# Three output projections from high and low parts, modulation chunks in value jobs, a bias pair ahead, the last expert reordered

## What is computed

```python
for i in range(DEPTH):                      # first block: 32 experts, top 2, FF 256
    h = rms_norm(x, norm1_g[i])             # i=0 gated MLP mixer, i=1 latent attention
    ...
    x = x + jnp.concatenate([mix, mem_out], axis=-1) @ w_out      # 1536 x 1024
    x = x + hierarchical_moe(rms_norm(x, norm2_g[i]), ...)
for i in range(DEPTH):                      # second block: 16 experts, FF 256
    mod = (silu(c) @ w_ada[i] + b_ada[i]).reshape(b, 6, d)
    sh_m, sc_m, g_m = mod[:, 0, None, :], mod[:, 1, None, :], mod[:, 2, None, :]
    sh_f, sc_f, g_f = mod[:, 3, None, :], mod[:, 4, None, :], mod[:, 5, None, :]
    hm = rmsnorm(x, norm_mix[i]) * (1 + sc_m) + sh_m
    # i=0 dilated mixer (w_in 1024 x 9216), i=1 forgetting mixer (w_in 1024 x 3088)
    x = x + g_m * (attention_output @ w_out)                      # 1024 x 1024
    hf = rmsnorm(x, norm_ffn[i]) * (1 + sc_f) + sh_f
    x = x + g_f * hierarchical_moe_2(hf, ...)
```

## Time and profile before

| | us |
|---|---|
| median of 3 runs | 1722.71 |
| lowest, highest | 1720.19, 1725.01 |
| the profiled execution | 1724.17 |
| its span | 1722.4 |
| PE busy in it | 1565.0 (91%) |
| DVE busy | 812.5 (47%) |
| ACT busy | 506.7 (29%) |
| POOL busy | 135.8 (8%) |

### The profile page before, as it was taken

The page is one execution under the profiler, slowest core; times in us unless marked ns, Lnnn a source line. Parts: engine busy times, 40 slices in busy tenths (PEclk is TensorE's granted clock), DMA queues, the critical chain, the costliest instruction groups (busy, mean ns, idle before and its releaser), DMA issues. The chain is left out here.

```text
span 1722.4 us, 23229 instructions
## 1 busy us (share of the span) xinstructions
PE 1565.0 (91%) x8906; PEld 986.1 (57%) x8906; DVE 812.5 (47%) x1862; ACT 506.7 (29%) x1016; POOL 135.8 (8%) x158
## 2 busy tenths in 40 slices
PE   6899899999699798999979988997899979889997
PEld 3487455554375555555437766776565537646553
DVE  0647343333433636333236745664663336576433
ACT  1222121111215412111116555654222125641211
POOL 0000201010000002010001001000021001002110
PEclk9899999999899999999999989998989989998999
DMA  9785559999872083999996350335357993616794
GB/s 358 259 340 217 199 237 420 421 421 421 359 285 106 4 366 132 421 420 421 420 425 252 147 202 24 142 121 222 123 222 314 421 390 122 244 73 273 286 420 199
DMA packets 62107, 467.23 MB, mean 271 GB/s; under 512 B 7664, under 2 KB 15776, under 8 KB 17184
## 3 DMA queue, kind: packets, MB, share of 16 engines
q1 hardware_dynamic: 61984, 465.59, 66.9%
HBM read 462.81 MB, written 2.76 MB: 270 GB/s over the span
## 5 line engine op out<-in xcount | busy, mean ns | idle before, releaser
L1528 PE MATMUL PS<-ring,catT 128*64 128x256 f32 x3072 | 368.5, 383 | 16.1 <-DMA ring<-in_moe 8.7
L1528 PEld LDWEIGHTS PS<-ring,catT 128*64 128x64 f32 x3072 | 213.3, 137 | 187.2 <-issue 81.8
L783 PE MATMUL PS<-w_split,h_split 128*128 128x512 f32 x1152 | 275.5, 397 | 10.0 <-DVE w_split L868 10.0
L783 PEld LDWEIGHTS PS<-w_split,h_split 128*128 128x128 f32 x1152 | 214.2, 189 | 65.0 <-DVE w_split L868 17.0
L1550 PE MATMUL PS<-ring,hidden_cols 128*64 128x512 f32 x768 | 181.3, 593 | 0.2 <-DMA ring<-in_moe 0.2
L868 DVE TENSOR_TENSOR w_split<-ring,w_split 128x512 fp32r<-128x512 f32 x192 | 131.6, 705 | 75.8 <-ACT w_split L816 75.5
L1791 DVE SCALAR_TENSOR_TENSOR xn_split<-PS,slot_w,xn_split 128x512 fp32r<-128x512 f32 x96 | 72.1, 751 | 189.8 <-ACT xn_split L1644 189.8
L816 ACT CAST w_split<-ring 128x512 fp32r<-128x512 f32 x192 | 118.2, 620 | 113.4 <-PE PS L783 112.9
L1653 ACT ACTIVATE hidden_rows<-PS 128x128 f32<-128x128 f32 x96 | 26.7, 278 | 413.3 <-PE PS L1528 413.3
L1561 PE MATMUL PS<-xn_split,back 64*128 64x512 f32 x768 | 114.4, 416 | 13.4 <-DVE xn_split L1791 13.4
L1644 ACT ACTIVATE xn_split<-PS,slot_w 128x512 fp32r<-128x512 f32 x96 | 66.0, 687 | 154.4 <-PE PS L1550 154.4
(11 more groups left out here) (411 smaller groups left out, 1822.2 us busy)
## 6 DMA issues: line engine op xcount, KB each, us to landing
ring<-in_moe SPq DMA_DIRECT2D x288, 1024.0 KB, 14.7
ring<-in_w_ada SPq DMA_DIRECT2D x16, 3072.0 KB, 12.1
ring<-in_a_w_in SPq DMA_DIRECT2D x23, 2048.0 KB, 9.7
ring<-in_b_w_in SPq DMA_DIRECT2D x8, 2048.0 KB, 18.1
ring<-in_a_w_out SPq DMA_DIRECT2D x2, 3072.0 KB, 11.4
ring<-in_b_w_out SPq DMA_DIRECT2D x2, 3072.0 KB, 10.6
ring<-in_w_mem_kv SPq DMA_DIRECT2D x2, 2048.0 KB, 12.3
ring<-in_a_w_out SPq DMA_DIRECT2D x2, 2048.0 KB, 8.8
```

The costliest lines, as they stand in the source:

```text
L783: last = nc.tensor.matmul(PS[:, 2 * (i % 2) + t, :], hs[:, hp, k, t * P:(t + 1) * P], wk[:, (KT * i + k) % splits, wp, :], start=k == 0 an ...
L1528: last = nc.tensor.matmul(PS[half * WIN:(half + 1) * WIN, 4 + e % 2, 0:2 * P].rearrange("p (g f) -> p g f", g=2), xf[:, e % 2, k, :], gate ...
```

## The change

- `b_w_out`, `a_w_out_2` and `b_w_out_2` go through a new function, `project_out`. Source and weights are split: ACT makes the highs (of two source blocks and one weight tile per tile at first), POOL the lows of three weight tiles in four, DVE every fourth and all source lows. PE makes six fp32r matmuls for each tile, over both token halves, with four slots of weight tiles. The ada steps are spread over the tiles of their chunk, and the ada chunk is freed after the last tile. DVE adds half 0 of the columns to x after the first tile of chunk 1, half 1 at the end. The gate rows are copied by ACT, after the fourth tile.
- Three ada chunks (numbers 10, 11 and 13) move from the last two output projections into the value jobs of `project_heads_split`: one step or none behind a tile's low part. PE's sums for them come two tiles before the end of the last job. `a_w_out_2` has one ada chunk left for three, `b_w_out_2` two for three.
- The biases of pairs 0 and 1 are both loaded in the projection's block (twelve loads for six); the attention loads from pair 2 on.
- In the MoE's last expert PE does `down(e)` before `combine(e-1)`, and DVE `take_turned(e)` before `low(e-1)`.

```diff
+        def ada_chunk():
+            ada_at.append(len(stream.chunks))
+            stream.add([ada_aps[len(ada_at) - 1]])
...
-        c_ain2 = weight("a_w_in_2", 8, [512] * 18)
-        c_aout2 = weight_amid("a_w_out_2", 8, [512] * 2, [1, 2])
+        c_ain2 = []
+        for half in range(2):
+            c_ain2.append(len(stream.chunks))
+            stream.add(chunk_aps(A["a_w_in_2"], 8, [512] * 18)[9 * half:9 * half + 9])
+            ada_chunk()
+        c_aout2 = weight_amid("a_w_out_2", 8, [512] * 2, [1, 0])
         c_moe2 = experts("moe2", 16)
         c_bin2 = weight("b_w_in_2", 8, [512] * 3 + [16] + [512] * 3)
-        c_bout2 = weight_amid("b_w_out_2", 8, [512] * 2, [1, 2])
+        ada_chunk()
+        c_bout2 = weight_amid("b_w_out_2", 8, [512] * 2, [1, 1])
...
+        def ada_step(dve, c, part, k):
+            w = stream.view(ada_at[c], 8)
+            if k == 0:
+                dve.wait_ge(*stream.landed(ada_at[c]))
+                dlink(nc.vector.tensor_scalar(part, w[:, 0, :], silu_c[:, 0:1], None, ALU.mult))
+            else:
+                dlink(nc.vector.scalar_tensor_tensor(part, w[:, k, :], silu_c[:, k:k + 1], part, ALU.mult, ALU.add))
         def ada_part(dve, c, part, give_back=True):
-            dve.wait_ge(*stream.landed(ada_at[c]))
-            w = stream.view(ada_at[c], 8)
-            dlink(nc.vector.tensor_scalar(part, w[:, 0, :], silu_c[:, 0:1], None, ALU.mult))
-            for k in range(1, KT):
-                dlink(nc.vector.scalar_tensor_tensor(part, w[:, k, :], silu_c[:, k:k + 1], part, ALU.mult, ALU.add))
+            for k in range(KT):
+                ada_step(dve, c, part, k)
...
+        def project_out(k, first, ada, gate, router, after):
+            place = [first + c + sum(ada[:c + 1]) for c in range(2)]
             ada0 = sum(at < first for at in ada_at)
+            n_ada = sum(ada)
+            tiles = 2 * k
+            with ExitStack() as st:
...
+                block = st.enter_context(nc.Block())
+                def on_dve(n):
+                    return n % 4 == 3
                 @block.sync
                 def _(sp):
+                    wr, br = router_weights(router)
+                    nc.sync.dma_start(wr, A[f"wr{router}"]).then_inc(r_loaded.sem, 16)
+                    nc.sync.dma_start(br, A[f"br{router}"].partition_broadcast(P)).then_inc(r_loaded.sem, 16)
+                    stream.issue(nc, sp, first + 2 + n_ada)
                 @block.tensor
                 def _(pe):
                     if gate is not None:
                         for j in range(KT):
                             last = nc.tensor.matmul(PS[:, 6 + j // 4, (j % 4) * P:(j % 4 + 1) * P],
                                                     gate[:, j:j + 1].to_broadcast([P, P]), ident[:], start=True, stop=True)
                         last.then_inc(gate_made.sem, 1)
+                    for n in range(tiles):
+                        c, j = n // k, n % k
+                        if c == 0:
+                            pe.wait_ge(*s_low.at(j + 1))
+                        if on_dve(n):
+                            pe.wait_ge(*w_low_dve.at(n // 4 + 1))
+                        else:
+                            pe.wait_ge(*w_low_pool.at(n - n // 4 + 1))
+                        for t in range(TT):
+                            for i, (sp_, wp) in enumerate(((0, 0), (0, 1), (1, 0))):
+                                last = nc.tensor.matmul(PS[:, 2 * c + t, :], sr[:, sp_, j, t * P:(t + 1) * P], wk[:, n % 4, wp, :],
+                                                        start=j == 0 and i == 0, stop=j == k - 1 and i == 2)
+                        last.then_inc(w_used.sem, 1)
+                    pe.wait_ge(*part_ready.at(1))
+                    if gate is not None:
+                        pe.wait_ge(*gate_taken.at(1))
+                    ada_sums(n_ada, part).then_inc(ada_made.sem, 1)
                 @block.scalar
                 def _(act):
+                    nc.scalar.activation(stat[:, 2, 30:31], ones_f[:, 0:1], ACT.Sqrt)
+                    for n in range(tiles):
+                        c, j = n // k, n % k
+                        if 2 * n < k:
+                            for h in (2 * n, 2 * n + 1):
+                                nc.scalar.copy(sr[:, 0, h, :], catT[:, h, :]).then_inc(s_high.sem, 1)
+                        if j == 0:
+                            act.wait_ge(*stream.landed(place[c]))
+                        if n >= 4:
+                            act.wait_ge(*w_used.at(n - 3))
+                        nc.scalar.copy(wk[:, n % 4, 0, :], stream.view(place[c], k)[:, j, :]).then_inc(w_high.sem, 1)
+                        if gate is not None and n == 3:
+                            act.wait_ge(*gate_made.at(1))
+                            nc.scalar.copy(grow[:], PS[:, 6:8, :].rearrange("p b n -> p (b n)")).then_inc(gate_taken.sem, 1)
+                @block.gpsimd
+                def _(pool):
+                    for n in range(tiles):
+                        c, j = n // k, n % k
+                        if j == 0:
+                            pool.wait_ge(*stream.landed(place[c]))
+                        if not on_dve(n):
+                            pool.wait_ge(*w_high.at(n + 1))
+                            nc.gpsimd.tensor_tensor(wk[:, n % 4, 1, :], stream.view(place[c], k)[:, j, :], wk[:, n % 4, 0, :].bitcast(F32),
+                                                    ALU.subtract).then_inc(w_low_pool.sem, 1)
                 @block.vector
                 def _(dve):
+                    def add_columns(c):
+                        dve.wait_ge(*w_used.at(k * (c + 1)))
+                        nc.vector.sem_inc(chunk_used, 1)
+                        for t in range(TT):
+                            ps, r = PS[:, 2 * c + t, :], x[:, t, c * BANK:(c + 1) * BANK]
+                            if gate is not None:
+                                dve.wait_ge(*gate_taken.at(1))
+                                dlink(nc.vector.tensor_tensor(ps, ps, grow[:, c * BANK:(c + 1) * BANK], ALU.mult))
+                            nc.vector.tensor_tensor(r, r, ps, ALU.add)
                     done = 0
+                    for n in range(tiles):
+                        c, j = n // k, n % k
+                        if c == 0:
+                            dve.wait_ge(*s_high.at(j + 1))
+                            nc.vector.tensor_tensor(sr[:, 1, j, :], catT[:, j, :], sr[:, 0, j, :].bitcast(F32), ALU.subtract).then_inc(s_low.sem, 1)
+                        if j == 0:
+                            dve.wait_ge(*stream.landed(place[c]))
+                        if on_dve(n):
+                            dve.wait_ge(*w_high.at(n + 1))
+                            nc.vector.tensor_tensor(wk[:, n % 4, 1, :], stream.view(place[c], k)[:, j, :], wk[:, n % 4, 0, :].bitcast(F32),
+                                                    ALU.subtract).then_inc(w_low_dve.sem, 1)
+                        if ada[c]:
+                            for i in range(j * KT // k, (j + 1) * KT // k):
+                                ada_step(dve, ada0 + done, part[:, done, :], i)
+                            if j == k - 1:
+                                nc.vector.sem_inc(chunk_used, 1)
                                 done += 1
+                                if done == n_ada:
+                                    nc.vector.sem_inc(part_ready.sem, 1)
+                        if n == k:
+                            add_columns(0)
+                    add_columns(1)
+                    dve.wait_ge(*ada_made.at(1))
+                    dlink(nc.vector.tensor_copy(ada_out[:, 6 * ada0:6 * (ada0 + n_ada)], PS[:, 7, 0:6 * n_ada]))
+                    after()
...
+                part = catT[:, 8:11, :].rearrange("p k n -> p (k n)")
+                steps = KT * (len(jobs) - turns[-1] - 1) - splits - 2
...
-                    stream.issue(nc, sp, chunk(len(jobs)))
+                    stream.issue(nc, sp, chunk(len(jobs)) + 1)
...
+                            if i == len(jobs) - 1 and k == KT - 2:
+                                pe.wait_ge(*part_ready.at(1))
+                                pe.wait_ge(*taken_b.at(len(turns)))
+                                ada_sums(1, part.unsqueeze(1)).then_inc(ada_made.sem, 1)
...
+                            n = KT * (i - turns[-1] - 1) + k - splits
+                            if 0 <= n < steps:
+                                for j in range(n * KT // steps, (n + 1) * KT // steps):
+                                    ada_step(dve, ada, part, j)
+                                if n == steps - 1:
+                                    nc.vector.sem_inc(part_ready.sem, 1)
...
-                    for i in range(1, n):
-                        if i >= 2:
-                            sp.wait_ge(*logits_ready[1].at(2 * (i - 1)))
+                    for i in range(2, n):
+                        sp.wait_ge(*logits_ready[1].at(2 * (i - 1)))
```

(33 more changed lines are left out.)

131 lines of the change are left out of this document (20 added, 111 removed).

## The result

The changed kernel takes 1738.32 us in the median (1736.96 to 1742.43), against 1721.45 for the kernel before, run beside it: a ratio of 1.0096, with a 95% interval from 1.0067 to 1.0124. It is slower by some 17 us. The forecast was 1727.0 with a range up to 1737.0, so the time lies just outside, and on the side that had 0.38 of the chances. The profiled execution took 1739.65 us for a span of 1737.9.

What follows compares the result with a forecast made beforehand. PE was busy 1565 of 1722.4 us, but each touched stage was read separately. 15.5 - 3.6 + 2.6 + 4.1 + 1.0 - 8 - 9.1 + 1.7 = +4.2 on 1722.7, said as 1727.0; range 1711 to 1737.

Steps and rivals of the forecast that it cites:

- the side that had 0.38 of the chances: Whole kernel: the outcome slower, over 1727.9 us, given a chance of 0.38.
- Port: Output projections: two-input operations of POOL and DVE block each other, so tiles take 1.88 or 2.16 us, 1.56 without source lows.
- Rival B: Output projections: POOL and DVE don't block each other and PE sets the pace; 1702.8 us, chance 0.12.
- The late chunk: b_w_out: chunk 1 waits for the ada chunk freed after the twelfth tile; PE waits some 10 us, +15.5 us.
- Last expert: End of each MoE: down no longer waits for combine; -2.28 us for each of four, -9.1 in all.
- bias: Dilated attention: loading two pairs' bias ahead removes the wait for pair 1's; -8 us, from -6 to -14.
- Rival E: First two MoEs: the last down waits for its w_down piece, so the reorder gives nothing there; 1731.6 us, chance 0.08.
- Rival C: Dilated attention, pair 1: PE's idle time gets so short that the clock stays up; -7.8 us, 1719.2, chance 0.20.
- Ada chunks in the value jobs: Value jobs: three ada chunks' steps cost 0 in two big stages, +1.0 us in the fox projection; PE's sums +4.1.
- Restarts: PE restarts with the clock down after long waits: +1.7 us for the b_w_out stall, 0 at the projections' starts.
- Rival D: b_w_out: the half clock holds after the restart until the projection's end; +12.2 us, 1739, chance 0.10.

Runs made afterwards that it cites:

- experiment 3: The changed kernel with all weight lows of the three output projections made on DVE, none on POOL: 1716.61 us, ratio 0.9980 to the kernel before.
- experiment 4: The changed kernel with POOL's two-input subtraction in the output projections replaced by a one-input multiplication by 0.0, leaving out some products: 1715.36 us in one execution.
- Experiment 2: The changed kernel with b_w_out's first ada chunk worked through and given back in the first four tiles: 1729.49 us, ratio 1.0053 to the kernel before.
- experiment 1: The changed kernel with the old fp32 output projections back in all three places, other parts kept: 1691.94 us, ratio 0.9831 to the kernel before.
- Experiment 5: The changed kernel with PE kept busy by idle products of zeros ahead of its waits and at the end of the output projections: 1730.52 us, ratio 1.0057.
- experiment 10: The changed kernel with all weight lows on DVE, b_w_out's first ada chunk done in four tiles, six idle products behind the ada sums: 1707.32 us, ratio 0.9912.
- experiment 11: The changed kernel with the old fp32 output projections and six idle products of zeros behind each one's ada sums: 1690.83 us, ratio 0.9807 to the kernel before.
- experiment 12: The changed kernel with 36 tiny idle DVE copies ahead of DVE's wait for b_w_out's second chunk: 1737.87 us, ratio 1.0080 to the kernel before.
- experiment 9: The changed kernel with the old fp32 projections for a_w_out_2 and b_w_out_2 only, b_w_out still split: 1714.51 us, ratio 0.9964 to the kernel before.
- experiment 6: The kernel before with only the last expert reordered, down ahead of combine and take_turned ahead of low: 1715.55 us, ratio 0.9976.

## Why the prediction was wrong

**Port.** Right in kind, and in `b_w_out` in size. The forecast had 1.88 us a tile in its chunk 0 and 1.56 in chunk 1; measured 1.81 and 1.63. In chunk 0 of `a_w_out_2` it was 2.60 for 2.16, in the two chunks of `b_w_out_2` 2.17 and 2.14 for 2.16 and 1.85. POOL's low took 1.58 us in the mean beside DVE, and DVE's operations 0.2 to 0.5 us more each; experiments 3 and 4 show that they block each other, for the most part by POOL's second input. The shorter holds in the forecast's sum (0.85 for an ada step of 1.02) are estimates that no row shows. Rival B (1702.8) is out.

**The late chunk.** Right: issued 25.1 us into the block (forecast 25.6), a wait of 10.94 us, the block +15.1 (forecast +15.5). Experiment 2 shows the cause. `a_w_out_2` and `b_w_out_2` came out at -2.3 and +2.2 (forecast -3.6 and +2.6), without DMA waits.

**Last expert, bias.** -8.0 for -9.1, where the last MoE lost 1.7 of it to a slow first expert; -7.3 for -8. Rival E fell: only 0.43 us of waiting for the piece is left. Rival C did not happen in either half: the twelve transposes behind the wait took 1.54 us for each six again, after 2.24 us of idle time. (These are pair 0's last ones; DVE adds pair 1's bias ahead of normalising them, so the forecast's "pair 1" for this stretch was loosely named.)

**Ada chunks in the value jobs.** +6.8 for +5.1.

**Restarts.** The step that failed. It had 1.7 us for the restart in `b_w_out` and nothing else. Of that 1.7 at most half was there: the chunk took 19.53 us, 0.8 over the 18.7 of the sum (12 x 1.56), with its first 6.2 us at 0.50 and PE busy without a gap behind them. The block's end came 2 us ahead of the forecast with its restart, so the 1.7 goes out of the account below. And the step asked only whether the slow matmuls at the start of a projection can be hidden, and not what comes behind its end. There, PE does the 12 or 24 small sums and then stands for 1.0 to 2.5 us, and the granted clock falls. The two later routers, whose PE is on the path, ran at 0.50 for nearly all of their first 20 us, the first for half of them: +1.2, +2.8 and +2.8, and +1.7 in the first expert of the last MoE. That is 8.5 us. Of each 2.8, 1.7 is there with plain fp32 too (experiment 1: 34.8 for 33.1). Experiment 5 takes back the 5.6 of the two later routers, and six products of zeros behind the sums are enough for it (experiments 10 and 11). The +1.7 belongs to the one profiled execution: experiments 2 and 12, without fillers, have 108.7 us there. That the first router's +1.2 has the same cause is not shown; with fillers it kept 0.7 of it. The earlier trace rows held the sign: the 16 transposes ahead of the two routers took 3.65 and 3.56 us in the kernel before, where experiment 5 has them at 1.94. Part of the fall was there before, and the forecast took it for a constant. Rival D's time (1739) is near the measured one by chance: the second chunk of `b_w_out` ran its 72 records in 19.53 us, against the 18.7 of the sum, and the clock was back 6.2 us after the restart.

**Code.** +3.6 at the end of the second MoE, in no step of the forecast. It comes with the split `b_w_out` (experiment 9); its cause stays open (experiment 12).

8.5 - 1.7 + 3.6 makes 10.4 of the 11.3 us between the forecast sum (+4.2) and the difference of the spans (+15.5). The rest are the small misses above (the last MoE's 1.7 is counted once, in the 8.5), the forgetting attention (+1.2), and a start that was 2.1 us shorter.

Some of the forecast's own sums don't come out, by amounts that change nothing here: four tiles of DVE alone at k=12 make 4.8 us, not 5.1; 5.2 + 8 x 2.16 makes B+22.5, not B+23.7; PE's wait for chunk 1 by its own times is 12 us, not 10; and rival B's end at B+50 goes by 1.56 us a tile, where that rival has 1.4, so it is some 2 us too late.

The forecast also never compared the split with its own alternative. The edits that remove the DMA waits in the two last projections work as well with fp32, and better: 31.9 and 33.0 us against 40.0 and 42.2.

## What to carry to other kernels

Before a product is split into cheaper ones, sum up what must feed it per tile on each engine, and add DVE and POOL where POOL's operations have two inputs from SBUF; here a tile of 1.36 us in place of 1.72 got fed in 1.4 to 2.6. When steps that free a buffer are spread out to fit gaps, look for who waits for that free: here a transfer of 10.5 us. And price each part of a bundle against the bundle without it: here one part cost 46 us and hid that the others gave 29.

## What was not expected of the hardware

PE can be busy for 15 us on end and still be granted 1.2 GHz (1275 to 1290 in the changed kernel). Where fillers kept the clock up behind the projections, four other stages got 1.3 to 1.7 us longer (experiment 11); and with no filler at all the falls stood in other places in experiment 6. A one-input operation of POOL (128x512, 1.70 us in the mean, 1.48 at its shortest) is slower than its subtraction alone (1.27 at its shortest), yet leaves most of DVE's ada steps and weight lows at their own times; the source lows still took 0.66 us for 0.42. And some 36 more instructions on DVE made a stall of 5.34 us vanish, with another, of 3.41 us on PE, in its place.
